# The inverse inside a chunkwise delta rule: five doublings on 64-token chunks in place of four on 32-token blocks and a join

## What is computed

```python
def step(state, inp):
    r_t, w_t, k_t, v_t, kk_t, a_t = inp
    sa = jnp.einsum('bhij,bhj->bhi', state, -kk_t)
    state = (state * w_t[:, :, None, :]
             + sa[..., None] * (kk_t * a_t)[:, :, None, :]
             + v_t[..., None] * k_t[:, :, None, :])
    y_t = jnp.einsum('bhij,bhj->bhi', state, r_t)
    return state, y_t
...
y = (rwkv7_scan(r_h, decay[:, :, 0], k_dir[:, :, 0], v_h, kk, a[:, :, 0], False)
     + rwkv7_scan(r_h, decay[:, :, 1], k_dir[:, :, 1], v_h, kk, a[:, :, 1], True))
```

## Time and profile before

| | |
|---|---|
| median of 3 runs | 1900.05 us (1899.35 to 1900.52) |
| the profiled execution, its own time | 1895.41 us |
| its span | 1893.6 us |
| TensorE busy | 1745.7 us (92%), 16002 matmuls |
| VectorE busy | 1027.7 us (54%) |
| ScalarE busy | 700.6 us (37%) |
| instruction transfers (queue q8) | 127 packets, 2.08 MB |

### The profile page before, as it was taken

One profiled execution on the slowest core, in us unless ns is written; L12 is line 12 of the kernel. 1 busy time (PEld: TensorE's weight loads), 2 busy tenths in 40 slices (PEclk: granted clock), 3 DMA queues, 4 the chain that ended last, 5 costly groups with the idle time before them and its releaser, 6 DMA issues. The chain is left out here.

```text
span 1893.6 us, 36433 instructions
## 1 busy us (share of the span) xinstructions
PE 1745.7 (92%) x16002; PEld 1358.4 (72%) x16002; DVE 1027.7 (54%) x1469; ACT 700.6 (37%) x1059; POOL 113.4 (6%) x133
## 2 busy tenths in 40 slices
PE   7999688888887999999999988999888989999997
PEld 5666566766666678888888767886356768888885
DVE  6767455454532665776676575224787354443433
ACT  4344433232311644423231544234665344232312
POOL 2000000000000011000111110001200100000001
PEclk9999898989888999999999999999999989999999
DMA  5212221101002534443656222231000223223221
GB/s 199 67 56 68 96 70 35 37 20 36 28 18 107 176 121 145 155 156 134 233 189 213 74 81 68 77 123 47 1 1 2 100 67 100 101 89 100 97 94 55
DMA packets 49183, 172.16 MB, mean 91 GB/s; under 512 B 5553, under 2 KB 6961, under 8 KB 48257
## 3 DMA queue, kind: packets, MB, share of 16 engines
q1 hardware_dynamic: 39184, 133.31, 20.5%
q0 software_dynamic: 9840, 36.51, 5.7%
HBM read 161.15 MB, written 8.65 MB: 90 GB/s over the span
## 5 line engine op out<-in xcount | busy, mean ns | idle before, releaser
L366 PE MATMUL pair<-h_hi,w_hi 128*128 128x512 f32 x1032 | 417.4, 404 | 32.9 <-DVE w_lo L404 15.5
L367 PE MATMUL pair<-h_lo,w_hi 128*128 128x512 f32 x1032 | 405.4, 393 | 0.0
L368 PE MATMUL pair<-h_hi,w_lo 128*128 128x512 f32 x1032 | 405.3, 393 | 0.0
L404 DVE TENSOR_TENSOR w_lo<-w_raw,w_hi 128x1024 fp32r<-128x1024 f32 (+2 forms) x225 | 266.0, 1184 | 213.6 <-ACT w_hi L389 213.5
L389 ACT CAST w_hi<-w_raw 128x1024 fp32r<-128x1024 f32 (+2 forms) x225 | 221.8, 989 | 224.8 <-PE pair L368 220.3
L366 PEld LDWEIGHTS pair<-h_hi,w_hi 128*128 128x128 f32 x1032 | 196.0, 190 | 92.2 <-DVE w_lo L404 31.4
L367 PEld LDWEIGHTS pair<-h_lo,w_hi 128*128 128x128 f32 x1032 | 196.2, 190 | 42.6 <-issue 3.8
L368 PEld LDWEIGHTS pair<-h_hi,w_lo 128*128 128x128 f32 x1032 | 195.8, 190 | 41.9
L366 PE MATMUL pair<-ff_f_hi,w_hi 128*128 128x512 f32 x512 | 199.7, 390 | 0.5 <-DVE w_lo L404 0.5
L368 PE MATMUL pair<-ff_f_hi,w_lo 128*128 128x512 f32 x512 | 199.2, 389 | 0.0
L367 PE MATMUL pair<-ff_f_lo,w_hi 128*128 128x512 f32 x512 | 199.2, 389 | 0.0
(11 more groups left out here) (431 smaller groups left out, 2533.5 us busy)
## 6 DMA issues: line engine op xcount, KB each, us to landing
w_raw<-in_w_ff SPq DMA_DIRECT2D x128, 512.0 KB, 3.3
mod_w<-in_w_mod POOLq DMA_DIRECT2D x48, 512.0 KB, 3.6
w_raw<-in_w_in SPq DMA_DIRECT2D x22, 512.0 KB, 3.3
w_raw<-in_w_gate SPq DMA_DIRECT2D x16, 512.0 KB, 3.4
w_raw<-in_w_out SPq DMA_DIRECT2D x16, 512.0 KB, 3.3
w_raw<-in_w_rwkv SPq DMA_DIRECT2D x15, 512.0 KB, 3.3
w_raw<-in_w_da SPq DMA_DIRECT2D x12, 512.0 KB, 3.4
g_spill<-norm_pair POOLq DMA_DIRECT2D x16, 256.0 KB, 2.7
```

Source lines behind the costliest of these rows:

```text
L366: nc.tensor.matmul(out, w_hi, x_hi, start=(k == 0), stop=False)
L367: nc.tensor.matmul(out, w_hi, x_lo, start=False, stop=False)
L368: last = nc.tensor.matmul(out, w_lo, x_hi, start=False, stop=(k == kt - 1))
L404: nc.vector.tensor_tensor(lo[:, s % SPLIT_SLOTS, 0:cols], pr.raw[:, w % RAW_SLOTS, 0:cols], hi[:, s % SPLIT_SLOTS, 0:cols].bitcast(F32), A ...
```

## The change

The inverse works on whole chunks. Every product of a level is 16 matmuls of 64x64 a direction instead of 32 of 32x32; both output halves of a PSUM bank become one area of 512 columns, so that each eviction, copy and transpose handles 512 elements a partition instead of 256. The join is a fifth level, with VectorE's masked eviction for its first product; its second product takes E as the stationary operand and goes straight to `Y64`. `gram_l` is 16 matmuls of 64x64 a direction. The masks are made anew, and `M`, `Y64` and `Z` share other buffers.

```diff
@@ gram_l
-                            for h, side in ((0, 0), (1, 0), (d, 1)):
-                                left = (2 * b + cc) * CH + 32 * h
-                                right = (2 * b + cc) * CH + 32 * (h ^ side)
-                                for hh in range(2):
-                                    at = 512 * hh + 256 * d + 128 * side + 32 * b
-                                    last = nc.tensor.matmul(out[rows32(2 * cc + h), at:at + 32], a["Bh"][rows64(hh), left:left + 32],
-                                                            a["Kt"][rows64(hh), right:right + 32], start=True, stop=True)
+                            cols = slice((2 * b + cc) * CH, (2 * b + cc + 1) * CH)
+                            for hh in range(2):
+                                at = 512 * hh + 256 * d + 64 * b
+                                last = nc.tensor.matmul(pr.pair[3][rows64(cc), at:at + 64], a["Bh"][rows64(hh), cols],
+                                                        a["Kt"][rows64(hh), cols], start=True, stop=True)
@@ TensorE, the levels
-                    for lev in range(1, 5):
+                    for lev in range(1, 6):
...
-                                for r in range(4):
-                                    last = nc.tensor.matmul(pr.bank[d][rows32(r), q * 32:(q + 1) * 32], a["Lc"][rows32(r), 0, q, :],
-                                                            a["X"][rows32(r), q, :], start=True, stop=True)
+                                for cc in range(2):
+                                    last = nc.tensor.matmul(pr.bank[d][rows64(cc), q * 64:(q + 1) * 64], a["Lc"][rows64(cc), q, :],
+                                                            a["X"][rows64(cc), q, :], start=True, stop=True)
...
+                            left, right = (a["Y"], a["E"]) if lev < 5 else (a["E"], a["Y"])
                             for q in range(8):
-                                for r in range(4):
-                                    last = nc.tensor.matmul(pr.bank[d][rows32(r), 256 + q * 32:256 + (q + 1) * 32], a["Y"][rows32(r), q, :],
-                                                            a["E"][rows32(r), q, :], start=True, stop=True)
+                                for cc in range(2):
+                                    last = nc.tensor.matmul(pr.bank[d][rows64(cc), q * 64:(q + 1) * 64], left[rows64(cc), q, :],
+                                                            right[rows64(cc), q, :], start=True, stop=True)
@@ ScalarE
-                            nc.scalar.copy(flat(a["X"][:, :, :]), pr.bank[d][:, 256:512]).then_inc(s["xout"], 1)
+                            nc.scalar.copy(flat(a["X"][:, :, :]), pr.bank[d]).then_inc(s["xout"], 1)
...
-                        nc.scalar.mul(flat(a["M5"][:, :, :]), pr.bank[d][:, 0:256], -1.0).then_inc(s["m5out"], 1)
...
+                        nc.scalar.copy(flat(a["Y64"][:, :, :]), pr.bank[d]).then_inc(s["y64"], 1)
@@ VectorE
-                            nc.vector.tensor_tensor(a["E"][:, :, :], pr.bank[d][:, 0:256].rearrange("p (q t) -> p q t", q=8),
-                                                    level[:, d, lev, :].unsqueeze(1).to_broadcast([P, 8, 32]), ALU.mult)\
-                                .then_inc(s["eout"], 1)
+                            nc.vector.tensor_tensor(a["E"][:, :, :], pr.bank[d].rearrange("p (q t) -> p q t", q=8),
+                                                    wide(level[:, lev, :]), ALU.mult).then_inc(s["eout"], 1)
```

More of the change, by code:

```diff
@@ L94, in shape_constants @@
     out["keep"] = np.broadcast_to((t % CH != 0).astype(f), (P, T))
[L96 removed]
+    t64 = np.arange(64)[None, :]
     before = [lambda row, col: row < col, lambda row, col: row > col]
[L98 to L99 removed]
+    parts = [before[d](i[:, None] % 64, t64).astype(f) for d in range(2)]
     parts += [(before[d](i[:, None] % 64, t64) | (i[:, None] % 64 == t64)).astype(f) for d in range(2)]
[L101 to L108 removed]
+    own = i[:, None] % 64 == t64
+    for n in (1, 2, 4, 8, 16, 32):
+        joined = (i[:, None] % 64 // (2 * n) == t64 // (2 * n)) & (i[:, None] % 64 // n != t64 // n)
+        parts.append(own.astype(f) - joined.astype(f))
     out["rw_masks"] = np.concatenate(parts, 1)
@@ L1110, in _ @@
-                            last.then_inc(s["px"], 1)
-                        beside(p, 2 * lev - 1)
-                        gates.pe(pe, point + 2 * lev - 1)
-                    for d, a in both(p):
-                        pe.wait_ge(s["xout"], 2 * (4 * p + 3) + d + 1)
-                        for q in range(8):
-                            for cc in range(2):
-                                first, second = rows32(2 * cc + d), rows32(2 * cc + 1 - d)
-                                last = nc.tensor.matmul(pr.bank[d][second, q * 32:(q + 1) * 32], a["Lc"][first, 1, q, :],
-                                                        a["X"][first, q, :], start=True, stop=True)
-                        last.then_inc(s["m5"], 1)
@@ L1135, in _ @@
+                            last.then_inc(s["px"] if lev < 5 else s["y5"], 1)
+                        if lev < 5:
+                            beside(p, 2 * lev - 1)
+                            gates.pe(pe, point + 2 * lev - 1)
                     beside(p, 9)
```

95 lines of the change are left out of this document (25 added, 70 removed).

## The result

The changed kernel takes 1867.7 us (1863.24 to 1869.0, 4 runs), the kernel before beside it on the same chip 1899.7 us; the ratio is 0.983 [0.981, 0.986]. It is faster by 32 us where 11 were forecast. Beside the experiments the kernel before ran 42 times more, in 1884.4 to 1902.1 us with medians of 1891.5 to 1895.8, so the 32 us stand at the upper end: against those medians 24 to 28 us are left. Its times go with its granted clock, 0.962 in the slowest of the 42 and 0.973 in the fastest; the changed kernel's four runs have 0.980 to 0.982.

The account below looks back on a forecast made before the run. The inverse parts were taken as nearly bound by delivery of TensorE's instructions. Terms +29 - 3 - 28 + 4 + 1 - 14 = -11 us on 1895.4 gave 1884.4 profiled, 1889 us with the median's 4.6; range 1868 to 1912.

Parts of the forecast that it names:

- TensorE bounds these parts, and its gaps are the delivery of instructions: Inverse parts: TensorE waits for program blocks of about 256 instructions, delivered in about 3.55 us each.
- the rival that the gaps were something else: Inverse parts: gaps are not delivery, or do not shrink with the instruction count; +31 us, 1931 us, 4% chance.
- Products and join, +29: Four pairs: 64x64 products take 1.94 us instead of 1.20, the join 4.0 instead of 2.6; +29 us.
- `gram_l`, -3: `gram_l`: 256 loads instead of 768, 4.5 us instead of 7.3; -3 us.
- Gaps, -28: Inverse parts: 31 us of TensorE's gaps between instruction blocks should close, 3 us left; -28 us.
- `begin`, +4: `begin` on VectorE takes longer, so TensorE waits about 1 us for direction 1 in each pair; +4 us.
- L988, +1: Second level: evictions delay L1345, for which L988 waits, by 0.25 us in three pairs; +1 us.
- VectorE's late work: Other VectorE growth was to stay beside TensorE; the rival put half of 24 us on its path, +12, 1901 us, 17%.
- Clock, -14: Inverse parts: 56 us at half speed cost up to 28; with gaps closed a third was left; -14 us.
- All gaps close and the clock stays at full speed: Rival: -3 us more for gaps and all 28 of the clock's instead of 14; -28, 1872 us, 13% chance.

Follow-up runs that it names:

- e5: Changed kernel with each 64x64 matmul of both products cut into two of 32 output rows, all 64 moving columns kept: 1890.11 us, 0.996.
- e13: e12 with its small matmul done twice, for both halves, so 128 of 32x32 in each of 24 products: 1884.20 us, 0.996.
- e3: Changed kernel with VectorE's part of the gate step put ahead of its other work in the fifth level: 1858.97 us, 0.981.
- e7: e3 with TensorE doing slot 0 of the next pair's `prepare` between the first products of the two directions: 1857.73 us, 0.980.
- e9: e11 with only 32 of the 64 moving columns sent in the 24 products of levels 2 to 4: 1889.76 us, 1.001.
- e11: Control: changed kernel whose 24 products of levels 2 to 4 read `Lc` and a constant block, same shape, no inverse computed: 1871.39 us, 0.989.
- e12: e11 with the 24 products of levels 2 to 4 as 64 matmuls of 32x32 weights and 32 moving columns: 1849.93 us, 0.978.
- e10: e11 with only 32 of the 64 output rows computed in the 24 products, all 64 moving columns kept: 1870.01 us.
- e1: Changed kernel with each 64x64 matmul of both products of a level cut into two of 32 moving columns: 1965.93 us, 1.035.

## Why the prediction was off

*TensorE bounds these parts, and its gaps are the delivery of instructions: right.* e5 doubles the number of instructions in a product at the same 1.9 us of TensorE time, and 25 us of breaks return, some 256 instructions apart. That spacing, and e13's breaks with the small tiles, speak against the rival that the gaps were something else. The packets came as forecast, 105. The rule of the Trainium skill, "Runtime: NRT & Kernel Launch", "Instruction fetch mechanics", that slow dispatch mostly hides the crossing into a new block does not hold for these short matmuls.

*Products and join, +29: right at full clock.* 1.94 us a product, and 3.9 for the join's two.

*`gram_l`, -3: right.* L1023 takes 4.2 us where L1034 took 7.3.

*Gaps, -28: too small.* The six groups of the earlier trace rows went from 43.7 to 14.2 us of "issue", -30; about 15 had been forecast to stay. More closed in lines that I had left out of the sum: the two other groups of L1059 had 4.3 us of "issue" ahead of them and the join's two lines 4.9. From the first product to the end of the loop TensorE's idle time fell by 23.5 us, although 6.5 at the join and 5.6 for `begin` were added, so some 36 us closed: 8 more than forecast.

*`begin`, +4: 6.* The waits are 1.40 us for direction 1 and a little more in front of the first pair; the group of L1086 has 7.8 us of waiting for the transpose in place of 2.2. The transpose of 512 elements took 0.71, as estimated. *L988, +1: 0.*

*VectorE's late work, left at nothing in the forecast: +6.5.* The rival had the mechanism, one engine's order at one place, but the wrong place. It stood behind the join, where the fifth eviction was added: VectorE has to wait for the join's first product before it can do it, and the gate step's part is queued behind. In the kernel before that wait was there too in the first pair, 1.04 us long, but not in the other three. e3 measured it by taking it away. e7 shows the opposite case, a wait that moves to the next one when filled.

*Clock, -14: this is the step that failed.* The forecast said that where the gaps close, "most of the half-speed stretches have nothing to start behind", and left a third. In the inverse parts half-speed time went from 56 to 11 us, in the parts between from 12 to 1. At 0.43 us each, a price measured with e9's products and so an estimate here, the 56 us that went are 24 us, 10 more than forecast. By the clock the outcome is nearest to the rival "All gaps close and the clock stays at full speed", which had 13% and 1872 us.

The reason given was half of it. Every stretch at half speed does begin behind idle time. But the gaps didn't have to go for the stretches to go: the changed kernel still has 14 gaps of 1 us or more for 22, and one stretch for 13; e5 has 20 such gaps and three stretches. And what stands behind a gap sets how long the clock stays down: behind the same wait of 1.5 us it was 3.4 us with 64 moving columns and 27.3 with 32 (e11, e9), and behind one of 1.7 us it was 17.1 with small tiles (e12). So the clock came back mainly because the products became larger, with 64 moving columns, and only in small part because TensorE stopped waiting: with the breaks put back, half-speed time over all executions grew by 3 us with large tiles (e5) and by 9 with small ones (e13).

Beyond these, 5 us of the gain lie behind the loop over pairs, where the forecast had nothing; one piece may be a half-speed stretch of the kernel before at 683 to 686 us that is absent after. No experiment touched that. The sum of what was missed: 10 of clock, 8 of gaps, 5 behind the loop and 1 at L988, less 6.5 at the join and 2 at `begin`, is 15.5 of the 21 us between 1884.4 forecast and 1863.24 profiled. The rest is not assigned.

Still open: small products in 24 of 40 bring the half-speed time from 7 us (e11) to 34 (e12), where the kernel before has 56. The rest may come from level 1, the join and `gram_l` in small blocks, which these kernels kept large, or from gaps together with them. No run here separates that. Nor does any say why one gap is followed by a half-speed stretch and another of the same length is not.

Best version: e3 and e7, 1858.97 and 1857.73 us, are ahead of the kernel before by 1.9 and 2.0%. Against the changed kernel their spans are 6.2 and 4.6 us less and their medians 9 and 10, but the intervals touch (e7 [0.978, 0.981], changed [0.981, 0.986]) and they were not timed side by side: a gain over the changed kernel of some 0.3 to 0.5% is likely, not settled. Of the two e3 is the simpler.

## What to carry to other kernels

When TensorE runs short matmuls, count instructions as a cost of their own: look for breaks inside runs of equal matmuls and count from one to the next. A larger tile that costs more TensorE time at full clock can win twice, by fewer instructions and by a clock that stays up; treat these as two terms, each with its own experiment, and don't derive one from the other. Before you say that a clock fell without a gap, read the time just ahead of the fall as well as the stretch itself. Where an operation is added to one engine's queue, ask what stands behind it there and who waits for that.

## What was not expected of the hardware

- Half the work was slower: 32 moving columns through 64x64 weights in 24 products cost 18 us more than 64 columns (e9, e11), at the same pace per matmul while the clock was up; the clock stayed down for 27.3 us in place of 3.4 behind the same wait.
- A pair of load and matmul took 29 to 30 ns with 64x64 weights and either 64 or 32 moving columns (1.94 us for 64, 3.77 for 126), 28 ns with 64x32 weights written to two groups of 32 output rows (e10, 1.82 us for 64), and 14 to 15 ns with the same weights written to all four (e5, 1.38 us for 94). L1048's 64x64 products, which spread over four corners, took 17.5 ns (0.56 us for 32). What sets these paces was not tested.
- 37.5 us in one piece at 1.2 GHz with TensorE busy throughout, begun behind a gap of 1.49 us (e1).
- In 92 of 92 cases a stretch at half speed began with 0.9 us or more of idle time in the 4 us ahead of it, while most gaps of 1 us or more had no such stretch behind them (14 gaps and one stretch in the changed kernel).
